# An output projection over halves of the tokens instead of whole rows, with the final norm of the left half placed inside it

## The reference, cut to what matters

```python
merged = g_a * (y_a @ w_proj_a[layer]) + g_b * (y_b @ w_proj_b[layer])
x = x + merged @ w_out[layer]          # the output projection
...
return rmsnorm_2(x, g_final)           # x / sqrt(mean(x*x) + eps) * g_final, per token
```

## Time and profile before

| | us |
|---|---|
| median of 3 runs | 2383.28 |
| lowest and highest of them | 2382.28, 2384.09 |
| the profiled execution, its own time | 2381.16 |
| its span, first to last instruction | 2379.4 |
| PE busy in that span | 2347.2 (99%) |
| mean granted TensorE clock in the span | 0.996 of full speed |

### The profile page before, as it was taken

One profiled execution on the slowest core, in us unless ns is written; L12 is line 12 of the kernel. 1 busy time (PEld: TensorE's weight loads), 2 busy tenths in 40 slices (PEclk: granted clock), 3 DMA queues, 4 the chain that ended last, 5 costly groups with the idle time before them and its releaser, 6 DMA issues.

```text
span 2379.4 us, 29871 instructions
## 1 busy us (share of the span) xinstructions
PE 2347.2 (99%) x11080; PEld 1936.6 (81%) x11080; DVE 1283.4 (54%) x1791; ACT 860.8 (36%) x1293; POOL 801.3 (34%) x539
## 2 busy tenths in 40 slices
PE   9999999999999999999999999999999999999997
PEld 6888888878888878888788888888888888878886
DVE  4444663764444442246745444677777777742444
ACT  4422232233233331133343223455555555542122
POOL 2222222365545532322455455312222112223231
PEclk9999999999999999999999999999999999999999
DMA  3111222232222242223221323432332232253223
GB/s 135 45 36 45 89 80 97 85 137 88 90 80 80 80 168 97 80 101 115 103 76 71 113 96 124 151 113 87 100 123 94 91 115 85 101 186 124 106 97 115
DMA packets 69167, 237.94 MB, mean 100 GB/s; under 512 B 8240, under 2 KB 10448, under 8 KB 68944
## 3 DMA queue, kind: packets, MB, share of 16 engines
q1 hardware_dynamic: 53136, 180.74, 22.6%
q10 hardware_dynamic: 15936, 55.88, 5.9%
HBM read 177.35 MB, written 59.24 MB: 99 GB/s over the span
## 4 chain that ended last, share of the span: by engine, by line
PE 92%; DVE 4%; issue 2%; DMA 1%; ACT 1%; SPq 0%; POOL 0%; DVEq 0%; ACTq 0%
PE dense L796 18%; PE dense L797 18%; PE dense L798 18%; PE dense L979 9%; PE dense L980 9%; PE dense L981 9%; PE aux L1116 2%; PE aux L1129 1%; PE aux L1128 1%; PE aux L1101 1%; PE aux L1100 1%; PE aux L1063 1%; PE aux L934 1%; DVE x_lo L1983 1%; DVE att_p_late L2232 0%
## 5 line engine op out<-in xcount | busy, mean ns | idle before, releaser
L690 POOL TENSOR_TENSOR w_lo<-w_raw,w_hi 128x512 fp32r<-128x512 f32 x246 | 367.3, 1513 | 1022.1 <-ACT w_hi L1200 1013.1
L796 PE MATMUL dense<-x_hi,w_hi 128*128 128x512 f32 x1456 | 595.5, 409 | 6.4 <-DVE x_lo L1755 2.9
L798 PE MATMUL dense<-x_hi,w_lo 128*128 128x512 f32 x1456 | 570.1, 392 | 0.0
L797 PE MATMUL dense<-x_lo,w_hi 128*128 128x512 f32 x1456 | 569.6, 391 | 0.0
L1200 ACT CAST w_hi<-w_raw 128x1024 fp32r<-128x1024 f32 x121 | 127.0, 1050 | 566.5 <-PE dense L798 564.0
L798 PEld LDWEIGHTS dense<-x_hi,w_lo 128*128 128x128 f32 x1456 | 274.1, 188 | 59.9
L796 PEld LDWEIGHTS dense<-x_hi,w_hi 128*128 128x128 f32 x1456 | 274.6, 189 | 57.2 <-issue 9.3
L797 PEld LDWEIGHTS dense<-x_lo,w_hi 128*128 128x128 f32 x1456 | 275.3, 189 | 46.4 <-issue 1.9
L726 POOL TENSOR_TENSOR w_lo<-w_sums,w_hi 128x512 fp32r<-128x512 f32 x144 | 231.7, 1617 | 233.3 <-ACT w_hi L1356 233.3
L979 PE MATMUL dense<-x_hi,w_hi 128*128 128x512 f32 x576 | 226.5, 393 | 4.9 <-DVE work L2054 2.7
L981 PE MATMUL dense<-x_hi,w_lo 128*128 128x512 f32 x576 | 224.3, 389 | 0.0
(11 more groups left out here) (275 smaller groups left out, 3747.4 us busy)
## 6 DMA issues: line engine op xcount, KB each, us to landing
w_raw<-weights SPq DMA_DIRECT2D x163, 512.0 KB, 4.1
w_raw_b<-weights SPq DMA_DIRECT2D x34, 512.0 KB, 4.2
kept_qkv<-work ACTq DMA_DIRECT2D x24, 512.0 KB, 3.1
kept_m<-work ACTq DMA_DIRECT2D x22, 512.0 KB, 2.6
work<-kept_m SPq DMA_DIRECT2D x22, 512.0 KB, 3.3
residual<-xT SPq DMA_DIRECT2D x16, 512.0 KB, 7.5
kept_x<-residual ACTq DMA_DIRECT2D x16, 512.0 KB, 2.7
att_q<-kept_qkv SPq DMA_DIRECT2D x32, 256.0 KB, 3.9
```

Of the source, the lines that this page charges most:

```text
L690: last = pool.tensor_tensor(WL[:, u.slot, at4], WR[:, u.slot, at4], WH[:, u.slot, at4].bitcast(f32), ALU.subtract)
L796: pe.matmul(dst, WH[:, u.slot, k], hi, start=(k == 0), stop=False)
L797: pe.matmul(dst, WH[:, u.slot, k], lo, start=False, stop=False)
L798: last = pe.matmul(dst, WL[:, u.slot, k], hi, start=False, stop=(k == nk - 1))
```

## The change

The 8 units over 1024 tokens become 16 *half units* over 512 tokens: first tiles 0 to 7 for the left half, then tiles 0 to 7 for the right. Each half unit is 8 groups of 3 matmuls. The weights of the eight tiles are loaded, split by ACT and split by POOL a second time for the second pass. Fetch, scaling, addition, squaring and accumulation go by half tiles, 16 of each. Half unit i (0 to 15) has half t = i // 8 and tile k = i % 8. Sums and spread of the left half stand inside half units 8 and 10; DVE multiplies all eight left tiles in its steps 10 to 13, and SP stores them in its steps 14 and 15. The sums of right tiles 0 to 6 stand inside half unit 15; those of tile 7 and the spread follow the last matmul. POOL and ACT multiply only right tiles 3 and 6. The final products of the right half, and who stores them, are as before. The core of the diff:

```diff
+RUN = UNITS + 8
...
-    return c
+    return c if c < UNITS else c - 8
...
@@ block.sync
             for k in range(KT):
-                if U_WO + k + 3 < UNITS:
-                    load(Unit(U_WO + k + 3))
-                fetch(d_x[k], evac, U_WO + k + 1)
-            for t in range(2):
-                tok = slice(t * HALF, (t + 1) * HALF)
-                for k in range(KT):
-                    if t and k in STORED_BY_ACT:
-                        continue
...
+            for i in range(2 * KT):
+                t, k = i // KT, i % KT
+                if U_WO + i + 3 < RUN:
+                    load(Unit(U_WO + i + 3))
+                tok = slice(t * HALF, (t + 1) * HALF)
+                fetch(d_x[k][:, tok], evac, U_WO + i + 1, tok)
+                if i >= 14:
+                    for k in range(4 * (i - 14), 4 * (i - 14) + 4):
+                        put(0, k)
+            for k in range(KT):
+                if k not in STORED_BY_ACT:
+                    put(1, k)
...
@@ block.gpsimd
-            splits(U_PA + 2, UNITS - U_PA - 2)
-            for t in range(2):
-                pool.wait_ge(rs, 6 + t)
...
+            splits(U_PA + 2, RUN - U_PA - 2)
+            pool.wait_ge(rs, 6)
+            for k in ENDED_BY_ACT:
+                dst = XR[:, k, HALF:S]
+                pool.tensor_tensor(dst, dst, R[:, HALF:S], ALU.mult).then_inc(fin_pool, 1)
...
@@ block.tensor
-            unit(Unit(U_WO), ready=(x_ready, 40))
-            units(U_WO + 1, 6)
...
+            def half_unit(i, between=None):
+                u, t = Unit(U_WO + i), i // KT
+                pe.wait_ge(w_hi, u.count(1))
+                pe.wait_ge(w_lo, u.count(1))
+                pe.wait_ge(evac, u.count(-1))
+                tok = slice(t * HALF, (t + 1) * HALF)
+                dst = PD[:, u.slot, tok]
+                for k in range(KT):
+                    if i == 0:
+                        pe.wait_ge(x_ready, 40 + k + 1)
+                    pe.matmul(dst, WH[:, u.slot, k], XH[:, k, tok], start=(k == 0), stop=False)
+                    pe.matmul(dst, WH[:, u.slot, k], XL[:, k, tok], start=False, stop=False)
+                    last = pe.matmul(dst, WL[:, u.slot, k], XH[:, k, tok], start=False, stop=(k == KT - 1))
+                    if k == KT - 1:
+                        last.then_inc(mm_done, 1)
+                    if between:
+                        between(k)
...
+            def end_sums(t, of):
+                pe.wait_ge(*((sq, SQ_END + 2 * KT) if of else (acc, SQ_END + (2 * KT - 1 if t else KT))))
...
+            def end_spread(t, bank):
                 pe.wait_ge(dg, 6 + t)
+                pe.matmul(PA[:, bank], ONES[:], WK[:, 1, t * HALF:(t + 1) * HALF], start=True, stop=True
                           ).then_inc(spr, 1)
...
+            beside_half = {8: beside(g6=[lambda: end_sums(0, 0)]), 10: beside(g2=[lambda: end_spread(0, 0)]),
+                           15: beside(g5=[lambda: end_sums(1, 0)])}
+            for i in range(2 * KT):
+                half_unit(i, beside_half.get(i))
+            end_sums(1, 1)
+            end_spread(1, 3)
+            end_spread(1, 2)
...
@@ block.scalar
             act.preload_act_table(ACT.Sqrt)
+            for i in range(2 * KT):
+                t, k = i // KT, i % KT
                 tok = slice(t * HALF, (t + 1) * HALF)
+                split(Unit(U_WO + i + 2))
+                if i >= 2:
+                    act.wait_ge(acc, SQ_END + i - 1)
+                act.wait_ge(evac, U_WO + i + 1)
+                act.activation(WK[:, 2 + i % 2, tok], XR[:, k, tok], ACT.Square).then_inc(sq, 1)
+                if i == KT:
+                    root(6, slice(0, 4))
+            root(7, slice(4, 8))
+            act.wait_ge(spr, 8)
+            act.copy(R[:, HALF:S], PA[:, 2]).then_inc(rs, 1)
+            gains()
...
@@ block.vector
+            for i in range(2 * KT):
+                u, t, k = Unit(U_WO + i), i // KT, i % KT
                 tok = slice(t * HALF, (t + 1) * HALF)
+                src = loaded(LD_X + i)[:, tok]
...
+                dve.scalar_tensor_tensor(src, src, vec(V_GF + k), R1[:, tok], ALU.mult, ALU.mult).then_inc(x_sc, 1)
+                dve.wait_ge(x_sc, KT + i + 1)
+                dve.wait_ge(mm_done, u.c + 1)
+                dve.tensor_tensor(XR[:, k, tok], PD[:, u.slot, tok], src, ALU.add).then_inc(evac, 1)
+                if i < 2 * KT - 1:
+                    add_square(SQ_END + i, k == 0, WK[:, 0, tok], WK[:, 2 + i % 2, tok])
+                if i == KT:
+                    dst = RT[:, 2, 0:4]
+                    dve.wait_ge(ss, 6)
+                    chain(dve.tensor_scalar(dst, PA[:, 1, 0:4], 1.0 / D, EPS, ALU.mult, ALU.add))
+                    dve.reciprocal(dst, dst).then_inc(rr, 1)
+                    diagonals(6, WK[:, 1], range(4))
+                if KT + 2 <= i < KT + 6:
+                    if i == KT + 2:
+                        dve.wait_ge(spr, 6)
+                    ended(0, range(2 * (i - KT - 2), 2 * (i - KT - 2) + 2))
...
+            dve.wait_ge(ss, 8)
...
+            diagonals(7, WK[:, 1], range(4, 8))
+            dve.wait_ge(spr, 7)
             ended(1, ENDED_BY_DVE)
```

More of the change, by code:

```diff
@@ L644, in _, with fetch @@
             used = []
-            def fetch(src, by, count):
+            def fetch(src, by, count, cols=slice(0, S)):
                 nonlocal n
@@ L650, in fetch @@
                 used.append((by, count))
-                sp.dma_start(WK[:, TMP + n % 2], src).then_inc(ld[n % 2], 16)
+                sp.dma_start(WK[:, TMP + n % 2, cols], src).then_inc(ld[n % 2], 16)
                 n += 1
@@ L667, in _, with put @@
             sp.dma_start(R1, d_r1[0]).then_inc(r1_in, 16)
-            for k in range(KT):
-                if U_WO + k + 3 < UNITS:
-                    load(Unit(U_WO + k + 3))
-                fetch(d_x[k], evac, U_WO + k + 1)
-            for t in range(2):
-                tok = slice(t * HALF, (t + 1) * HALF)
-                for k in range(KT):
-                    if t and k in STORED_BY_ACT:
-                        continue
[L677 to L681, removed]
+            def put(t, k):
+                if t and k in ENDED_BY_ACT:
+                    sp.wait_ge(fin_act, ENDED_BY_ACT.index(k) + 1)
+                else:
+                    sp.wait_ge(fin, KT + ENDED_BY_DVE.index(k) + 1 if t else k + 1)
+                tok = slice(t * HALF, (t + 1) * HALF)
+                sp.dma_start(out[k][:, tok], XR[:, k, tok]).then_inc(outs, 16)
+            for i in range(2 * KT):
[7 more added lines that the diff above has]
+                        put(0, k)
+            for k in range(KT):
+                if k not in STORED_BY_ACT:
+                    put(1, k)
             sp.wait_ge(outs, 16 * 2 * KT)
@@ L1170, in last_sums @@
+            def end_sums(t, of):
+                pe.wait_ge(*((sq, SQ_END + 2 * KT) if of else (acc, SQ_END + (2 * KT - 1 if t else KT))))
+                src = WK[:, 2 + (2 * KT - 1) % 2] if of else WK[:, 0]
+                for b in range(4):
+                    last = pe.matmul(PA[:, 1 - of, 4 * t + b:4 * t + b + 1],
+                                     src[:, (4 * t + b) * P:(4 * t + b + 1) * P], ONES[:, 0:1],
                                      start=True, stop=True)
                 last.then_inc(ss, 1)
-            def last_spread(t):
+            def end_spread(t, bank):
@@ L1193, in split @@
             def split(u):
-                if u.reg is None and u.c >= UNITS:
+                if u.reg is None and u.c >= RUN:
                     return
@@ L1719, in _ @@
                 hi_part(k, XR[:, k], 0.5)
[L1720 to L1727, removed]
             act.preload_act_table(ACT.Sqrt)
-            for t in range(2):
+            for i in range(2 * KT):
+                t, k = i // KT, i % KT
                 tok = slice(t * HALF, (t + 1) * HALF)
[L1731 to L1738, removed]
+                split(Unit(U_WO + i + 2))
[9 more added lines that the diff above has]
+            gains()
             for k in STORED_BY_ACT:
                 if k in ENDED_BY_ACT:
-                    act.wait_ge(fin_act, len(ENDED_BY_ACT) + ENDED_BY_ACT.index(k) + 1)
+                    act.wait_ge(fin_act, ENDED_BY_ACT.index(k) + 1)
                 else:
-                    act.wait_ge(fin, len(ENDED_BY_DVE) + ENDED_BY_DVE.index(k) + 1)
+                    act.wait_ge(fin, KT + ENDED_BY_DVE.index(k) + 1)
                 act.dma_start(out[k][:, HALF:S], XR[:, k, HALF:S]).then_inc(outs, 16)
@@ L2338, in _ @@
                 lo_part(k, XR[:, k], 40 + k + 1, 0.5)
[L2339 to L2349, removed]
             def ended(t, tiles):
@@ L2380, in _ @@
+            part, dst = RT[:, 0, 4:8], RT[:, 3, 4:8]
+            dve.wait_ge(ss, 7)
+            chain(dve.tensor_scalar(part, PA[:, 1, 4:8], 1.0 / D, EPS, ALU.mult, ALU.add))
+            dve.wait_ge(ss, 8)
```

(4 more changed lines are left out.)

18 lines of the change are left out of this document (6 added, 12 removed).

## The result

The changed kernel is slower by about 0.2%: 2387.52 us against 2382.39, both medians of 14 runs, ratio 1.0019 with a 95% interval of 1.0012 to 1.0026. (The ratios of this text are the measurement's own estimate from all runs; the quotient of the two medians is 1.0022.) I had forecast 2382.1 and no measurable change. Its profiled execution took 2386.85 us, span 2385.1.

What follows compares the result with a forecast made beforehand. PE was taken to bound the kernel, busy 99% of the span. Stream +1.0 and tail −2.2 gave −1.2 us on the profiled 2381.16, so 2380.0; with the median 2.1 above, 2382.1 us, range 2379.3 to 2387.0.

Steps and rivals of the forecast that it cites:

- Work removed and added in the stream: PE up to the last matmul: old sums, spreads and restarts go, −4.46 us; new sums and one spread come, +2.75.
- half units costing what units did: PE's matmuls: the same 384 matmuls and weight loads are issued, each half unit taking 5.44 us: 0 us.
- The wait in half unit 0: PE stalls 1.4 us, 1.5 with restart, for the low part of the eighth input tile.
- the steady pace: Half units 5.44 us apart: weights and x, fetched in 3.88 us, arrive before PE needs them, costing 0 us.
- rival C: Fetches with latency over 5.4 us delay half units; at 6.0, each second starts 0.6 late: about 2389 us, chance 0.09.
- rival B: Split, POOL, scaling, addition and square form a ring of 5.7 to 5.8 us against PE's 5.44: 2385.3 us, chance 0.28.
- The wait for the sums: In half unit 8 PE waits for the eighth left tile's square and accumulate: 0.7 to 1.7 us, taken as 1.2.
- the late kind of step: Alternate DVE steps where scaling waits for POOL, so the addition ends 5.1 us after a half unit's end, not 4.1.
- the lock: DVE's two-SBUF-input instructions and POOL exclude each other; DVE's half scalings sometimes take 1.9 us instead of 0.65.
- stalls leave the clock alone: PE's clock: an earlier stall of 2.72 us cost no long time at half clock, so nothing is counted for stalls of 1.5.
- The tail: After the last matmul: only eight stores are left, ending 12.9 us after it instead of 15.1, so −2.2 us.
- the spread's 1.1 us: After the last matmul DVE waits about 1.1 us for the spread, against 0.86 in the stream.

Runs made afterwards that it cites:

- The R1 run: The changed kernel, but ACT copies row R1 to two idle PSUM banks and DVE's scaling reads it there: 2385.14 us, ratio 1.0013.
- The filled gaps: The changed kernel with five idle matmuls before the last sums and five before the last spread: 2385.93 us, ratio 1.0017.

## Why the prediction was wrong

- **Work removed and added in the stream** (−4.46, +2.75), and half units costing what units did: right. With fetches ahead of loads the stream is 91.46 against 91.55; 2.75 + 1.5 − 4.46 gives −0.2.
- **The wait in half unit 0**: 1.3 against 1.4. Right.
- **"Both in time: 0 us", the steady pace**: this step failed. The latency of 3.88 that I worked out was right for most fetches (3.5 to 4.2), but I let it stand for all of them. Twice it was 5.5 or more, past the 5.4 that rival C names as its point, and PE lost 1.8 us of waiting, some 2.3 with restarts: 2.3 of the 3.5 us by which the stream missed. Beneath it lies the place of the fetch behind the load in SP's queue, which I had worked with and held to be harmless: with the two swapped, fetches over 5 us cost nothing. The size of the fetches was not it: 256 KB took 3.86 where full bandwidth gave 3.88, so what I had drawn from the rule on transfers under 1 MiB (the Trainium skill, DMA: Bandwidth & Descriptors, "Bandwidth"), that a half fetch gets less than its share of the gain, does not show here. My rows held the warning: the first fetch of the kernel before took 5.06 where others took 4.6, and I used it only to weigh rival B. A load of instructions was in flight beside that one too. The stage had two such loads before and has three with 16 half units written out on PE, and I never counted them.
- **The wait for the sums, 1.2**: mis-sized, 1.9, above the 1.7 of the late kind of step, on which tile 7 fell; that is 0.9 of the 3.5 us with the restart. The R1 run shows that most of it was the lock. And in two of four profiles the clock fell behind it, 1.2 us more. I had written that stalls leave the clock alone; that is refuted.
- **The ring (rival B)**: its parts are real, the lock above all, but the ring did not close for long: steps took turns, as I forecast, with some runs of late ones, and no half unit started late but the two after late fetches.
- **The tail, −2.2**: mis-sized, −1.2. The queue of stores shrank as I had said, but I carried over the spread's 1.1 us, when the same gap can end at half clock. The filled gaps gave 0.9 of the missing 1.0 back.
- **Range and chances**: as a difference I had −1.2 and measured +5.1; that the baseline of 14 runs lies 0.9 under that of the 3 runs I started from makes the miss look smaller in the total. The range ended at 2387.0, 0.5 short; slower by over 0.2%, at whose edge the result lies (ratio 1.0019), had 0.09. C was priced at +6.9, with every fetch late. I saw the mechanism and its threshold, and gave it little because no row beside a single load showed 5.4. What came was a few late fetches, a larger wait and a lower clock, and none of my cases had all three.

## What to carry to other kernels

When steps are cut in half, ask of each operand not how long its transfer takes but what its issue waits for: here x was queued behind a weight load that waits for POOL, harmless at 10.9 us a step and costly at 5.4, and swapping two lines in SP's queue took all of it back. A margin must hold for the slowest transfer in the trace, and code that is written out in a line brings transfers of its own. A stall of 2 us on PE can be charged twice, so it is worth moving sums and spreads one step later than they need to be.

## What was not expected of the hardware

- The same stall may or may not bring TensorE's clock down. Elsewhere in both programs there is a stall of 2.72 us, near 500 us. Before, the matmul behind it took 0.50 us; in the profile after, the granted clock was 0.72 in 503 to 505 and 0.50 in 505 to 507, on identical code. Six of the ten profiles show the fall behind this stall. It goes with when the last stage begins, as said above, and may be part of why one kernel's runs differ by 5 us; the share is open.
- A fetch of 256 KB went from 3.4 to 4.2 us to 5.2 to 6.1 with one 16 KB load of instructions in flight, in the twelve cases where the load began in the first 2.9 us of the fetch, and not in the five where it began in the last 0.6 us. No run takes the load away and leaves all else, and why 16 KB cost over 1 us is open.
